# Halved loads of an attention gate, products of a gate row at other places, and the low parts of eleven weights made by GpSimd, in a whole hybrid decoder layer

## What is computed

```python
def reference(x, c, positions, w_ada, b_ada, g_pre, w_in, ..., w_out, g_final):
    mod = jax.nn.silu(c) @ w_ada[l] + b_ada[l]
    shift, scale, gate = jnp.split(mod[:, None, :], 3, axis=-1)
    h = rmsnorm(x, g_pre[l]) * (1.0 + scale) + shift
    proj = h @ w_in[l]
    (c_q, c_kv, k_pe, gate_mla, q_ret, k_ret, v_ret, gate_ret,
     merge_mla, merge_ret) = jnp.split(proj, pts, axis=-1)
    y_mla = mla_branch(c_q, c_kv, k_pe, positions, g_q[l], w_q_up[l], g_kv[l], w_kv_up[l])
    y_mla = y_mla * jax.nn.silu(gate_mla)
    y_ret = retention_branch(q_ret, k_ret, v_ret, positions, g_ret[l]) * jax.nn.silu(gate_ret)
    merged = (jax.nn.sigmoid(merge_mla) * (y_mla @ w_proj_mla[l])
              + jax.nn.sigmoid(merge_ret) * (y_ret @ w_proj_ret[l]))
    x = x + gate * (merged @ w_out[l])
    return rmsnorm(x, g_final)
```

## Time and profile before

| | |
|---|---|
| median of 3 runs | 1579.26 us (1577.84 to 1579.91) |
| profiled execution, its own time | 1582.74 us |
| its span | 1580.9 us |
| TensorE busy | 1541.4 us (97%) |
| TensorE weight loads | 1289.0 us (82%) |
| VectorE busy | 970.1 us (61%) |
| ScalarE busy | 668.3 us (42%) |
| GpSimd busy | 458.4 us (29%) |
| mean granted TensorE clock | 0.994 of full |
| TensorE's share of the chain that ended last | 83% |

### The profile page before, as it was taken

The page is one execution under the profiler, slowest core; times in us unless marked ns, Lnnn a source line. Parts: engine busy times, 40 slices in busy tenths (PEclk is TensorE's granted clock), DMA queues, the critical chain, the costliest instruction groups (busy, mean ns, idle before and its releaser), DMA issues.

```text
span 1580.9 us, 20493 instructions
## 1 busy us (share of the span) xinstructions
PE 1541.4 (97%) x7472; PEld 1289.0 (82%) x7472; DVE 970.1 (61%) x1591; ACT 668.3 (42%) x1144; POOL 458.4 (29%) x388
## 2 busy tenths in 40 slices
PE   5999999999999999999999999999999999999998
PEld 4788888888888888788888888888778888878886
DVE  6884444444444448752566676666776776789644
ACT  7553355543333353342343343435554444445311
POOL 0032223332222200200344444454643343423000
PEclk9999999999999999999999999999999999999999
DMA  9343233332333334699577676657977777888432
GB/s 382 98 136 113 110 111 111 109 113 107 112 122 113 94 102 140 253 413 345 181 243 243 229 256 227 238 196 252 325 248 255 241 240 239 309 283 294 152 107 80
DMA packets 157316, 313.20 MB, mean 198 GB/s; under 512 B 12816, under 2 KB 87696, under 8 KB 148512
## 3 DMA queue, kind: packets, MB, share of 16 engines
q1 hardware_dynamic: 140384, 279.44, 50.7%
q0 software_dynamic: 4640, 16.84, 3.0%
q10 hardware_dynamic: 12192, 15.60, 3.0%
HBM read 201.47 MB, written 109.31 MB: 197 GB/s over the span
## 4 chain that ended last, share of the span: by engine, by line
PE 83%; DVE 5%; DMA 5%; issue 2%; ACT 2%; POOL 2%; ACTq 0%; SPq 0%; POOLq 0%; DVEq 0%
PE p_banks L2492 10%; PE p_banks L2452 10%; PE p_banks L2453 10%; PE p_banks L2450 10%; PE p_banks L2524 5%; PE p_banks L2365 2%; PE p_banks L2367 2%; PE p_banks L2366 2%; PE p_banks L2734 2%; PE p_banks L2602 2%; PE p_banks L2736 2%; PE p_banks L2764 2%; PE p_banks L2763 2%; PE p_banks L2737 2%; PE p_banks L2765 2%
## 5 line engine op out<-in xcount | busy, mean ns | idle before, releaser
L1923 DVE TENSOR_TENSOR w_form<-w_pair,w_form 128x512 fp32r<-128x512 f32 x150 | 116.2, 776 | 124.9 <-ACT w_form L1496 123.3
L1496 ACT ACTIVATE w_form<-w_pair 128x512 fp32r<-128x512 f32 x150 | 94.7, 632 | 217.1 <-PE p_banks L2453 211.7
L1578 ACT ACTIVATE prob<-p_banks,neg_max 128x128 f32<-128x128 f32 (+3 forms) x64 | 47.5, 742 | 187.4 <-DVE neg_max L2050 187.4
L2450 PE MATMUL p_banks<-h_hi,w_form 128*128 128x512 f32 x300 | 116.7, 389 | 0.0
L2452 PE MATMUL p_banks<-h_lo,w_form 128*128 128x512 f32 x300 | 116.7, 389 | 0.0
L2453 PE MATMUL p_banks<-h_hi,w_form 128*128 128x512 f32 x300 | 116.7, 389 | 0.0
L1219 POOL TENSOR_TENSOR w_pair<-w_pair 128x512 f32<-128x512 f32 x25 | 32.5, 1299 | 235.4 <-DVE w_form L1923 235.4
L2734 PE MATMUL p_banks<-t_hi,w_hi 128*128 128x512 f32 x224 | 88.2, 394 | 2.7 <-DVE t_lo L1691 2.7
L619 DVE TENSOR_TENSOR w_lo<-w_raw,w_hi 128x1024 fp32r<-128x1024 f32 (+3 forms) x63 | 69.8, 1110 | 30.2 <-ACT w_hi L598 29.6
L2736 PE MATMUL p_banks<-t_lo,w_hi 128*128 128x512 f32 x224 | 87.9, 392 | 0.0
L1305 POOL TENSOR_TENSOR qk_by_sine<-rotation_raw,rotation_table 128x512 f32<-128x512 f32 x32 | 41.9, 1310 | 158.4 <-DMA rotation_raw<-qk_chunks 110.9
(11 more groups left out here) (346 smaller groups left out, 4472.7 us busy)
## 6 DMA issues: line engine op xcount, KB each, us to landing
w_pair<-in_w_pairs SPq DMA_DIRECT2D x25, 1024.0 KB, 4.9
v_ret<-v_stage POOLq DMA_DIRECT2D x32, 512.0 KB, 5.7
v_chunk<-v_ret SPq DMA_DIRECT2D x32, 512.0 KB, 3.7
w_raw<-in_w_ret SPq DMA_DIRECT2D x28, 512.0 KB, 5.1
w_raw<-in_w_dense SPq DMA_DIRECT2D x23, 512.0 KB, 6.0
act_t<-stage SPq DMA_DIRECT2D x40, 256.0 KB, 2.0
act_t<-stage_late SPq DMA_DIRECT2D x40, 256.0 KB, 2.0
ada<-in_w_ada SPq DMA_DIRECT2D x4, 2048.0 KB, 24.8
```

The costliest lines, as they stand in the source:

```text
L1496: self.nc.scalar.activation(self.form[f % FORM_SLOTS][:, 0, :], self.form_source(f), ACT.Copy).then_inc(self.form_hi, 1)
L1923: nc.vector.tensor_tensor(self.form[f % FORM_SLOTS][:, 1, :], self.form_source(f), self.form[f % FORM_SLOTS][:, 0, :].bitcast(F32), ALU.su ...
L2450: self.nc.tensor.matmul(out, w_hi[:, cut], x_hi[:, q, :], start=fresh and q == 0, stop=False, skip_group_check=True)
```

## The change

Three things, in one edit:

1. `head_gate` is loaded in two halves of 512 columns. The half for a head's first two pairs is loaded when two pairs of the head before are done, the other when all four are. VectorE waits for a half at every second pair. SyncE issues 16 DMAs in place of 8.
2. The eight products of the gate row, one each in units 4 to 11 before, stand in units 4, 5, 6, 7, 8, 11 (two) and 12; its high and low parts are made in unit 13 rather than 12. SyncE's loads of the gate weights, at its units 3 to 10, and their waits for `gate_step` are as before.
3. All eleven `w_lo` that VectorE made within the retention are made by GpSimd (`lower_merge_weight`): the four of `MERGE_SPLIT` after the chunk of the step and before its set, six at the start of steps 12, 15, 19, 22, 26 and 29 before the chunk, and the last, which unit 2 of the product stage reads, after the last token sums. VectorE waits for that one in unit 0, before it makes the next.

```diff
--- before.py
+++ after.py
@@ -107,13 +107,13 @@
 T_PLACES = 4
 T_GROUPS = 4
 EARLY_TILES = 4
-YR_FROM, SECOND_FROM = 16, 64
+YR_FROM, SECOND_FROM = 16, 128
 OPERAND_FROM, T_FROM, W_SUMS_FROM, COPIED_FROM = (384, 384, 256, 256, 64, 64, 64, 64), 5, 100, 8
 C_FULL_FROM, RET_T_FROM = KD, (16 * KD, 16 * KD, 64, 64)
 PAIR_CHUNKS = NT // 2
 SUMS_FROM, OUT_HI_FROM, V_FIRST_FROM = 6, 11, 16
 GROUPS_SPLIT = ((0, 1), (2,), (3,), ())
-GATE_ROW_AT, GATE_ROW_UNIT = 4, 24
+GATE_ROW, GATE_ROW_DONE, GATE_ROW_UNIT = {4: (0,), 5: (1,), 6: (2,), 7: (3,), 8: (4,), 11: (5, 6), 12: (7,)}, 13, 24
 OUT_SPLIT = {15: (0,), 23: (1,), 25: (2, 3), 26: (4, 5), 27: (6, 7)}
 OUT_ORDER = (1, 3, 5, 7, 0, 2, 4, 6)
 SEQ += [("s", u) for u in range(RET_UNITS)]
@@ -875,7 +875,8 @@
         sp.wait_ge(self.w_lo_ready, R_V + V_PARTS)
         for slot in range(4):
             sp.wait_ge(self.stored[slot], 16 * PAIRS)
-        self.load_head_gate(sp, 0)
+        self.load_head_gate(sp, 0, 0)
+        self.load_head_gate(sp, 0, 1)
         self.load_qk(sp, 1)
         self.load_weight(sp, R_V + V_PARTS)
         sp.wait_ge(*self.done[SEQ.index(("q", H_MLA - 1))])
@@ -917,10 +918,11 @@
         for tiles, loaded in ((slice(0, 2), self.v_first_loaded), (slice(2, NT), self.v_loaded)):
             sp.dma_start(self.v[:, tiles, :, :].rearrange("p t l n -> p t (l n)").bitcast(F32), src[:, tiles, :]).then_inc(loaded, 16)
 
-    def load_head_gate(self, sp, h):
+    def load_head_gate(self, sp, h, half):
         if h:
-            sp.wait_ge(self.y_done, 4 * h)
-        sp.dma_start(self.head_gate[:, :], self.d["act_t"][h]).then_inc(self.head_gate_loaded[h % 2], 16)
+            sp.wait_ge(self.y_done, 4 * h - 2 + 2 * half)
+        cut = slice(half * HALF, (half + 1) * HALF)
+        sp.dma_start(self.head_gate[:, cut], self.d["act_t"][h][:, cut]).then_inc(self.head_gate_loaded[half], 16)
 
     def sync_attention(self, sp):
         d = self.d
@@ -939,8 +941,8 @@
                 sp.wait_ge(self.y_done, pair + 1)
                 sp.dma_start(d["y_mla"][head][:, 256 * q:256 * q + 256], self.y_full[:, pair % 2, :])\
                     .then_inc(self.y_stored[pair % 2], 16)
-                if q == NT // 2 - 1 and head < H_MLA - 1:
-                    self.load_head_gate(sp, head + 1)
+                if q % 2 and head < H_MLA - 1:
+                    self.load_head_gate(sp, head + 1, q // 2)
             if g % 2 == 0 and g // 2 <= CHUNK_STEPS:
                 self.move_rotation(sp, g // 2)
             if g == STEPS - 6:
@@ -1232,9 +1234,16 @@
                 units += 1
             if g % 2 and g // 2 < CHUNK_STEPS:
                 self.rotate_chunk(pool, g // 2)
+        done = 0
         for k in range(CHUNK_STEPS):
+            while done < self.set_units(k - 1):
+                if done % 2 and done > 1:
+                    self.lower_merge_weight(pool, R_MERGE + done // 2 + RING)
+                done += 1
             if k + 2 < CHUNK_STEPS:
                 self.lower_chunk(pool, k + 2)
+            if k in MERGE_SPLIT:
+                self.lower_merge_weight(pool, R_MERGE + MERGE_SPLIT.index(k))
             for part in SET0_SPLIT.get(k, ()):
                 self.lower_set(pool, part)
             if k % 2:
@@ -1242,6 +1251,7 @@
             if k == 3:
                 for unit in range(units, FILL_UNITS):
                     self.store_fill(pool, unit)
+        self.lower_merge_weight(pool, R_RET + RING - 1)
         self.gpsimd_output(pool)
 
     def lower_chunk(self, pool, n):
@@ -1254,6 +1264,12 @@
         pool.wait_ge(self.set_hi_ready, k + 1)
         self.nc.gpsimd.tensor_tensor(self.y_lo[k][:, :], self.y_raw[k][:, :], self.y_hi[k][:, :].bitcast(F32),
                                      ALU.subtract).then_inc(self.set_lo_ready, 1)
+
+    def lower_merge_weight(self, pool, r):
+        pool.wait_ge(self.w_hi_ready, r + 1)
+        pool.wait_ge(self.w_lo_ready, r)
+        self.nc.gpsimd.tensor_tensor(self.lo_place(r), self.raw_place(r), self.hi_place(r).bitcast(F32), ALU.subtract)\
+            .then_inc(self.w_lo_ready, 1)
 
     def token_sums(self, pool, k):
 
@@ -1720,7 +1736,7 @@
             if product < RET_PRODUCTS - 1:
                 for g in GROUPS_SPLIT[quad]:
                     self.high_t(act, product + 1, g)
-            if u == GATE_ROW_AT + KD:
+            if u == GATE_ROW_DONE:
                 act.wait_ge(self.gate_step, KD)
                 nc.scalar.activation(self.gate_hi[:, :], self.gate[:, :], ACT.Copy).then_inc(self.gate_step, 1)
             if product >= 4:
@@ -2053,8 +2069,8 @@
                 pair = (g - 4) // 2
                 h, q = divmod(pair, NT // 2)
                 dve.wait_ge(self.pv_done, pair + 1)
-                if q == 0:
-                    dve.wait_ge(self.head_gate_loaded[h % 2], 16 * (h // 2 + 1))
+                if q % 2 == 0:
+                    dve.wait_ge(self.head_gate_loaded[q // 2], 16 * (h + 1))
                 if pair >= 2:
                     dve.wait_ge(self.y_stored[pair % 2], 16 * (pair // 2))
                 elif pair == 0:
@@ -2159,8 +2175,6 @@
             cell = slice(s, s + 1)
             while units < self.set_units(n - 1):
                 self.merge_unit(dve, units)
-                if units % 2 and units > 1:
-                    self.lower_weight(dve, R_MERGE + units // 2 + RING)
                 units += 1
             dve.wait_ge(self.out_done, n + 1)
             nc.vector.bn_stats(self.stats[:, s, :], p[:, 4, :]).then_inc(self.stats_done, 1)
@@ -2194,14 +2208,11 @@
             if n == len(FILL_LATE) - 1:
                 for unit in range(FILL_UNITS - 2, FILL_UNITS):
                     self.lower_fill(dve, unit)
-            if n in MERGE_SPLIT:
-                self.lower_weight(dve, R_MERGE + MERGE_SPLIT.index(n))
             for g in T_SPLIT.get(n, ()):
                 self.low_t(dve, 0, g)
         self.low_t(dve, 0, T_GROUPS - 1)
         for unit in range(units, 2 * KD):
             self.merge_unit(dve, unit)
-        self.lower_weight(dve, R_MERGE + KD - 1 + RING)
 
     def lower_out_weight(self, dve, k):
         dve.wait_ge(self.out_hi_ready, OUT_HI_FROM + k + 1)
@@ -2225,13 +2236,15 @@
         for u in range(RET_UNITS):
             product, quad = divmod(u, QUADS)
             self.ret_outputs(dve, u)
+            if u == 0:
+                dve.wait_ge(self.w_lo_ready, R_RET + RING)
             self.lower_weight(dve, R_RET + u + RING)
             if product < RET_PRODUCTS - 1:
                 for g in GROUPS_SPLIT[quad]:
                     self.low_t(dve, product + 1, g)
-            if 0 <= u - GATE_ROW_AT < KD:
-                self.weigh_gate(dve, u - GATE_ROW_AT)
-            elif u == GATE_ROW_AT + KD:
+            for k in GATE_ROW.get(u, ()):
+                self.weigh_gate(dve, k)
+            if u == GATE_ROW_DONE:
                 dve.wait_ge(self.gate_step, KD + 1)
                 nc.vector.tensor_tensor(self.gate_lo[:, :], self.gate[:, :], self.gate_hi[:, :].bitcast(F32), ALU.subtract)\
                     .then_inc(self.gate_step, 1)
```

## The result

The changed kernel took 1590.08 us (median of 4 runs, 1589.04 to 1595.47) where the kernel before took 1579.15 us: a ratio of 1.0077, 95% interval [1.0053, 1.0101]. Measured again in another set, it was 1.0051 [1.0031, 1.0071]. It is slower, by 10.9 us between the medians here and by 6.8 in the other set (run e7), outside the range of the forecast. Its profiled execution is the longest of the four, 1595.47 us with a span of 1593.7, against 1582.74 and 1580.9 before.

The account below looks back on a forecast made before the run. TensorE, busy for 97% of the span, was taken to bound the kernel. -1.6 - 0.2 + 0.4 + 0.5 + 2.5 = +1.6 us on the median of 1579.26 gave 1580.9 us, forecast as no change; 8-in-10 range 1573.0 to 1586.0.

Parts of the forecast that it names:

- Gate row: Product stage: moved products shorten unit 12's stall but delay weight 15 and the merge tiles; +2.5 us (-2.5 to +5.5).
- +2.8 of wait, and with that +1.6 of clock: Product stage, unit 16: t_lo late behind the late merge tiles, TensorE waits 2.8 us, then loses 1.6 to the clock.
- Rival 3: Slower through SyncE's queue: merge tiles take 6.6 us, later operands stay behind TensorE; +4.6 us, 1583.9 us; chance 0.22.
- The expected gain in unit 12: Product stage: TensorE's 2.11 us stall shrinks to 1.2 and the clock stays full; -0.9 - 1.6 = -2.5 us.
- Head gate: Attention: with halves loaded earlier, both waits for late gate loads go; -1.6 us (0 to -1.85).
- Steps 2 to 10: Retention: the out_n stall goes, GpSimd makes sets 5 and 6 late by 0.9 and 3.1 us; together -0.2 us.
- Steps 12 to 29: Retention: GpSimd's low parts delay the chunk's subtraction that TensorE reads in step 22; +0.4 us (0 to +0.9).
- The last weight: Unit 2 of the product stage: GpSimd makes its low part 0.9 us late, partly swallowed in unit 12; +0.5 us.
- GpSimd as a whole: All eleven low parts moved to GpSimd: the terms -0.2, +0.4 and +0.5 us together, +0.7.
- The rule of the Trainium skill on two SBUF inputs: Retention: by it each moved subtraction could hold up a Vector t_lo or y_lo for 2.4 us; nothing was counted.
- The price of the clock: Anywhere on TensorE: a wait of over 2 us costs its length plus 1.6 us at half clock.

Follow-up runs that it names:

- e7: The changed kernel itself, unaltered, measured again in another set: 1.0051 of the kernel before.
- e2: The kernel before with the gate row's products moved alone: 1587.74 us, 1.0035 of before.
- e13: The changed kernel with the low part of the merge weights for unit 2 back on Vector: 1.0044 of the kernel before.
- e11: The kernel before with head gate halves, v_ret stores held back, eleven low parts on GpSimd, each merge weight behind its step's set: 1.0001 of before.
- e12: e11 with the low part for unit 2 back on Vector: 1578.77 us, 0.9982 of the kernel before.
- e8: e3 with GpSimd's v_ret stores held behind the first product of the next rotation, from attention step 54 on: 0.9993 of the kernel before.
- e10: The kernel before with the eleven low parts on GpSimd alone, each merge weight behind the set of its step: 1.0018 of before.
- e3: The kernel before with the head gate in halves alone: 1582.89 us, 1.0011 of before.

## Why the prediction was wrong

- **Gate row: the step that failed.** Forecast +2.5 us, measured alone +5.5 (0.0035 of 1581.6). Each link was right up to unit 16. The sum ended there: "+2.8 of wait, and with that +1.6 of clock", of which 1.5 us and no slow clock came. The measured cost stands at unit 20: 4.5 to 5.5 us and 3.6 us of clock in three profiles (e2, e13, the change), 1.5 us in e7's. Vector, some 5 to 6 us later against TensorE and nearly always busy, had nothing to catch up with; in unit 16 it had 4.8 us of room, in unit 20, behind three instructions that GpSimd's sums stretch before and after, only 0.4. Rival 3 named this ("the operands behind it stay behind TensorE", with long waits in units 16 to 20 as its sign) and priced it at 1.4 + 1.6 us. It should have been followed one product further, with each two-input Vector instruction that meets a GpSimd sum at 3.4 us, a price that the trace of the kernel before had too (t_lo at 1442.58 took 3.42 us, and was done 0.4 us before TensorE wanted it).
- **The expected gain in unit 12** (-2.5) can't be credited to the gate row. The wait went from 2.11 us to 1.44 without a slow clock after it (forecast 1.2), and to 0.44 in e2; but e1, the change without the gate move, has 1.55 with a full clock as well. Ten profiled kernels with all products at their old places have 0.4 to 2.4 us there, and eight of them a full clock. The prediction read one profile, of an execution above all four timed ones.
- **Head gate: the sign was wrong.** Forecast -1.6, measured alone +1.7. Both waits went, as said; the sentence that failed is that nothing else hung on it ("Eight more DMA issues on SyncE cost nothing on TensorE's path"). Being 2 us earlier turned round the order of loads at 1042. With the stores held it is -1.1 (0.9993), not told from nothing.
- **Steps 2 to 10: right** in mechanism and within 0.2 us in the waits for sets 5 and 6; the time that this part alone is worth was not measured.
- **Steps 12 to 29: the +0.4 didn't show.** There is no wait for qk_chunk at step 22 in the changed kernel.
- **The last weight:** +0.5 forecast; 2.7 us between e11 and e12, which differ in nothing else, and 1.1 us (0.0007) between the change and e13, in two sets. Its size is open.
- **GpSimd as a whole:** forecast -0.2 + 0.4 + 0.5 = +0.7, measured alone -1.4 [-2.8, -0.2].
- **The rule of the Trainium skill on two SBUF inputs** (SBUF - State Buffer, "Who interferes with whom"), which the forecast gave no weight, has Vector's instructions with two SBUF inputs contend with GpSimd's that read SBUF. The trace agrees with it: 3.42 and 3.38 us beside GpSimd's sums, 1.22 without. The moved subtractions of the retention did not bring this about: it stands in the product stage, in the kernel before too. What it decided is the room in unit 20, and, with the order of two starts, 2.2 us of the difference between the two profiles of the change.
- **The price of the clock**, 1.6 us for each wait of over 2 us, did not hold, see below.

## What to carry to other kernels

Before moving a producer later, list every queue whose waits count it, and read what stands behind those waits; here a DMA queue in program order held a weight, four operands and two tiles for a product that nobody needed yet. When a chain is late, follow it until an engine with idle time absorbs it, not until the first wait it causes, and compare at each product how much room the trace before had there (here 4.8 us, four units on 0.4). And where buffers of an in-order queue are shared by several engines, a saving of 2 us can change the order of transfers and cost more than it gave: look at what is issued within those 2 us.

## What was not expected of the hardware

The loss of clock behind a wait does not follow from the wait's length alone. In the kernel before 2.58 and 2.11 us were each followed by a window at 0.96. In e2 the same wait for out_n in step 6, 2.57 us, left its window at 1.00 (the first row below; e8 has 2.57 us and 1.00 too). In e10 a wait of 3.47 us left its window at 1.00 (above), in e2 4.5 us brought 0.91, and in e12, with 3.97 us, the window has 0.91 too (the last two rows):

```profile
1120.00:1160.00 40.00, 34.49 (x168) 26.57 (x167) 28.93 (x68) 20.82 (x39) 27.53 (x23) 1.00 0.87 312
...
1120.00:1160.00 40.00, 35.68 (x170) 29.04 (x169) 22.64 (x69) 20.43 (x39) 29.96 (x23) 0.91 0.88 310
...
PE p_banks L2545 <- POOL y_lo L1269: 4.3, 2, 4.0
```

So 1.6 us per wait of over 2 us was a price from two cases; the others show 0 to 3.6 us. And the change has 0.96 in 1080:1120, where its longest wait was 1.57 us; e3 has that wait too, and 1.00.

A load of 256 KB (rotation_raw) took 2.8 us in the kernel before (issued at 1041.56, ahead of the store and the v_head loads) and 7.7 us in e3 (1042.29), behind a 512 KB store and two v_head loads that went out within 0.8 us of it.
